# Moving the low parts of twelve weight blocks from VectorE to GpSimd in a decoder-trunk kernel

## The chip, the cores and the metric

The kernel runs on one core of a Trainium2 chip. The metric is the device time of one execution in microseconds; before the change it is 1524.93 us, the median of three runs (1524.68 to 1525.1). A profiled execution of the same kernel took 1524.4 us, of which 1522.7 us lie between its first and its last instruction.

## The reference

One inference step of a two-layer decoder trunk is computed for a prompt of 512 tokens and for 32 sample tokens (eight sequences of four), together 544 columns, with a model width of 1024. What matters here is the first mixer, a convolution layer:

```
h = rms(x, norm_mix)
a, g, mq = split(h @ w_in_a)               # 1024 -> 768, 768, 256
c = causal_dwconv(a * sigmoid(g), w, b)    # width 31, per channel
c = silu(layernorm(c))
m = mem_attend(rms(mq), mem_k, mem_v)
x = x + concat(c, m) @ w_out_a
```

After it come a gated feed-forward part, an attention layer with shared keys and values, and a second feed-forward part. All inputs and outputs are float32.

## The kernel before

**Blocks.** Every matrix product is cut into weight blocks of 1024 rows and 128 columns, which lie in SBUF as 128 partitions with 1024 elements each. The program numbers them: blocks 0 to 13 are `w_in_a` (0 to 11 alternate between a chunk of `a`, even, and the chunk of `g` that belongs to it, odd; 12 and 13 are the memory queries), and blocks from `S_MEM` = 14 on are the projections of the memory, then the output projection and the rest. To keep float32 accuracy, TensorE multiplies three times: high part of the weights by high and by low part of the activations, and low part of the weights by the high part (L532). One block of 544 columns is 48 matmuls.

**How a block gets ready.** SyncE loads it into one of four places of `w_raw` (L435; it waits until the low part of the block four places before is done). ScalarE copies it to the high part `w_hi` (L1151, `split_hi`), which waits for the load and for the matmuls of the block two before, since there are two places. VectorE subtracts, `w_lo = w_raw - w_hi` (L1600, `split_lo`), and the semaphore `w_lo_ready` counts that. TensorE waits for that count before each block.

**The order on the engines.** There is no scheduler; each engine's order is written out. In turn `s` VectorE takes the result of block `s` out of PSUM (L1669, into `glu_a`, `glu_g` or `tile_raw`), makes the low part of block `s + 2`, and does a fixed number of tap operations of the convolution (`conv(n)`, L1698 and L1700, 128x512 each). In odd turns it also makes `glu_lo` (L1712), the low part of a finished chunk of `a * sigmoid(g)`, of which ScalarE makes the high part `glu_hi` (L1236). TensorE needs both: it does 10 of the 31 taps itself as matmuls with diagonal matrices (L666, `conv_unit`), five of them beside each of the blocks 4 to 15. In odd turns `glu_ext` (L1815), `glu_new` (L1816) and a copy (L1818) follow, when the sigmoid of ScalarE is there (L1257), and then the sample tokens' taps (L1733, L1736, L1738).

**Turn 1** holds more: between blocks 1 and 2 TensorE transposes the memory rows (L612), the rows of the convolution state (L619) and of the feed-forward state (L626), VectorE copies them out of PSUM (L1827, L1831, L1837), and the squares of the memory are summed (L544).

**GpSimd** adds squares for the first norm (L2313, L2317), starts one DMA (L2337), and then waits for block 13's matmuls before it clears `mem_q_padded` (L2339) and loads cached memory keys.

Of the kernel before, what the change touches and what calls it, by code (L numbers as in the profile page):

```python
# [28 lines left out]
F32 = mybir.dt.float32  # L29
F32R = mybir.dt.float32r  # L30
I32 = mybir.dt.int32
ALU = mybir.AluOpType
# [41 lines left out]
S_MEM = S_IN + 2 * CC + MC  # L74
# [3 lines left out]
STEPS = S_FFN[1] + 68  # L78
# [8 lines left out]
def build(nc, a):  # L87
    ctx = ExitStack()
    with ctx:
        def sem(name):  # L90
            return ctx.enter_context(nc.semaphore(name))
# [4 lines left out]
        def place(name, shape, dt=F32, at=None):  # L96
            size = 4
            for n in shape[1:]:
                size *= n
            size = size + 31 & ~31  # L100
            if at is None:
                at = cursor[0]
                cursor[0] += size
            assert at + size <= nc.sbuf_usable_end, (name, at + size)
            h = nc.alloc_sbuf_tensor_at(name, shape, dt, offset=at)
            return h, at + size
# [10 lines left out]
        wraw, _ = place("w_raw", [P, 4, KD * P])  # L117
        whi, _ = place("w_hi", [P, 2, KD * P], F32R)
        wlo, _ = place("w_lo", [P, 2, KD * P], F32R)
# [113 lines left out]
        w_hi_ready, w_lo_ready = sem("w_hi_ready"), sem("w_lo_ready")  # L233
# [163 lines left out]
        def blocks_of(s):  # L397

            return HALF if S_OUT[1] <= s < S_FFN[1] else KD

        def mixed(i):

            return (0, 1, 2, 3, 6, 7, 4, 5).index(i) + 8


        turns = [(what, n) for _, what, n in sorted((g, what, n) for what in ("T", "OS", "KM", "XT", "XO", "KT", "KS", "KR")
                                                    for n, g in slots[what].items())]


        norms = [key for _, key in sorted([(8 * (s - S_B) + 12, ("tile", s)) for s, v in tiles.items()  # L410
                                           if s >= S_B and v[0] != "v"] +
                                          [(g, ("ov", h)) for h, g in slots["OV"].items()])]
# [1168 lines left out]
        def _(dve):  # L1581
# [10 lines left out]
            def split_lo(s, slot=None):  # L1592

                if slot is None:
                    if s >= STEPS:
                        return
                    slot = s % 4
                dve.wait_ge(w_hi_ready, s + 1)
                n = blocks_of(s) * P if isinstance(s, int) else KD * P
                nc.vector.tensor_tensor(wlo[:, slot % 2, 0:n], wraw[:, slot, 0:n], whi[:, slot % 2, 0:n].bitcast(F32),  # L1600
                                        ALU.subtract).then_inc(w_lo_ready, 1)
# [48 lines left out]
            for c in range(KD):  # L1650
                if c == PARAMS_AT:
                    split_lo(0)
                scaled_lo(xa_lo, xa_hi, c, xT[:, c, :], pcol("norm_mix", c), xg_hi, xg_lo, c + 1)
            split_lo(1)
            dve.wait_ge(sq_used, 8)
            root(psX[:, :, 0:HT], T, 1.0 / D, EPS, rstd[:, :])
# [134 lines left out]
            for s in range(0, S_MEM):  # L1791
                if s in tiles:
                    tile_take(s)
                    split_lo(s + 2)
                    conv(1)
                    side_conv(s)
                    tile_norm(s)
                    conv(5)
                    continue
# [502 lines left out]
        def _(pool):  # L2302
# [4 lines left out]
            def add_squares(norm, chunks=KD):  # L2307

                k = SQ[norm]
                if k:  # L2310
                    pool.wait_ge(sq_used, k)
                pool.wait_ge(sq_ready, k + 2)
                nc.gpsimd.tensor_tensor(total[:, :], sqt[:, 0, :], sqt[:, 1, :], ALU.add).then_inc(sq_used, 2)  # L2313
                for c in range(2, chunks - 1):
                    pool.wait_ge(sq_ready, k + c + 1)
                    pool.wait_ge(sq_used, k + c)
                    ins = nc.gpsimd.tensor_tensor(total[:, :], total[:, :], sqt[:, c % 2, :], ALU.add)  # L2317
                    ins.then_inc(sq_used, 1)
# [16 lines left out]

            add_squares("n0")
            pool.dma_start(a["s_conv_a"][0][:, 0:TAPS - 1 - DS, :], a["state_conv_a"][0][:, DS:, :]).then_inc(st_misc, 16)  # L2337
            pool.wait_ge(mm_done, S_MEM)
            pool.memset(qm[:, :, :], 0.0).then_inc(qm_zero, 1)  # L2339
            mem_cache_k(0)  # L2340
# [127 lines left out]
```

## Time and profile before

| | |
|---|---|
| median of three runs | 1524.93 us |
| the profiled execution | 1524.4 us |
| its span, first to last instruction | 1522.7 us |
| TensorE busy | 1419.0 us |
| VectorE busy | 953.9 us |
| ScalarE busy | 580.1 us |
| GpSimd busy | 154.3 us |
| low parts on VectorE (L1600) | 202 in 240.0 us |
| mean granted TensorE clock | 0.965 of full speed |

The sum in the prediction is made against the profiled execution, whose times run from the span's start. A granted clock of 1.00 is 2.4 GHz and of 0.50 is 1.2 GHz. In the timelines each row has a start, a time, the engine, the line and operation, and in brackets the idle time before it with what ended it. The time that a row of the timeline gives for several instructions is from the start of the first to the end of the last; starts follow each other somewhat before the end of the one before.

### The profile page before, as it was taken

To read this page: it belongs to the slowest core of one execution; us is meant where nothing else is said; L and a number is where in the kernel's file an instruction comes from. 1 tells how busy PE (TensorE), PEld (TensorE's weight loads), DVE (VectorE), ACT (ScalarE), POOL (GpSimd) and SP (SyncE) were. 2 spreads that over 40 slices of the span, in tenths; PEclk is the share of its full clock that TensorE was granted. 3 is DMA by queue.
4 is the path that set the end of the run, shared out by engine and by line. 5 is a ranking of instruction groups with operands and counts; after the bars stand their busy time and mean duration, and the time that the engine had idled before them with its cause. 6 is when DMAs were issued, how large, how long until landed. Compare 5 with 4: busy or idle time off the path is not lost.

```text
span 1522.7 us, 28281 instructions
## 1 busy us (share of the span) xinstructions
PE 1419.0 (93%) x11032; PEld 1348.2 (89%) x11032; DVE 953.9 (63%) x1825; ACT 580.1 (38%) x977; POOL 154.3 (10%) x202
## 2 busy tenths in 40 slices
PE   5899876989999999999999988888999999999997
PEld 4799874779999999999988877777899999999997
DVE  5788888556664466356776666666666536653652
ACT  3554433444342223222456545554443312221232
POOL 3000202303000000000210223320100000000001
PEclk8899987879999999999999999999999999999999
DMA  8121322214223233232222344332332322332322
GB/s 222 44 63 56 92 78 64 64 42 139 84 84 96 84 88 92 84 88 79 84 82 85 94 123 129 100 91 70 99 102 83 94 86 84 94 86 84 94 69 69
DMA packets 223216, 134.88 MB, mean 89 GB/s; under 512 B 7740, under 2 KB 216337, under 8 KB 223064
## 3 DMA queue, kind: packets, MB, share of 16 engines
q1 hardware_dynamic: 214687, 111.32, 25.3%
q0 software_dynamic: 7840, 21.89, 4.8%
q8 instruction: 72, 1.18, 0.3%
q10 hardware_dynamic: 584, 0.23, 0.1%
q14 instruction: 33, 0.26, 0.1%
HBM read 126.19 MB, written 7.85 MB: 88 GB/s over the span
## 4 chain that ended last, share of the span: by engine, by line
PE 72%; DVE 15%; ACT 7%; issue 4%; POOL 1%; ACTq 1%; DMA 0%; DVEq 0%; POOLq 0%
PE acc L532 59%; PE acc L709 3%; DVE conv_out L1698 2%; ACT w_hi L1151 2%; PE psX L666 1%; DVE w_lo L1600 1%; DVE softmax_stats L2089 1%; PE psT L666 1%; PE psX L544 1%; ACT exps L1462 1%; PE psX L796 1%; PE acc L544 1%; DVE root_row L1623 1%; ACT xa_hi L1173 1%; DVE psX L2087 1%
## 5 line engine op out<-in xcount | busy, mean ns | idle before, releaser
L532 PE MATMUL acc<-xa_hi,w_hi 128*128 128x272 f32 x1760 | 370.9, 292 | 5.4 <-DVE w_lo L1600 5.4
L532 PE MATMUL acc<-xa_hi,w_lo 128*128 128x272 f32 x1760 | 365.4, 289 | 0.0
L532 PE MATMUL acc<-xa_lo,w_hi 128*128 128x272 f32 x1760 | 364.3, 289 | 0.0
L1151 ACT ACTIVATE w_hi<-w_raw 128x1024 fp32r<-128x1024 f32 (+1 forms) x202 | 206.7, 1023 | 342.6 <-PE acc L532 311.6
L1600 DVE TENSOR_TENSOR w_lo<-w_raw,w_hi 128x1024 fp32r<-128x1024 f32 (+1 forms) x202 | 240.0, 1188 | 97.9 <-ACT w_hi L1151 96.3
L532 PEld LDWEIGHTS acc<-xa_hi,w_hi 128*128 128x128 f32 x1760 | 278.4, 190 | 11.7 <-DVE w_lo L1600 6.1
L532 PEld LDWEIGHTS acc<-xa_lo,w_hi 128*128 128x128 f32 x1760 | 278.1, 190 | 0.0
L532 PEld LDWEIGHTS acc<-xa_hi,w_lo 128*128 128x128 f32 x1760 | 276.1, 190 | 0.0
L532 PE MATMUL acc<-xb_hi,w_hi 128*128 128x272 f32 x896 | 194.6, 298 | 2.0 <-DVE xb_lo L2035 2.0
L532 PE MATMUL acc<-xb_hi,w_lo 128*128 128x272 f32 x896 | 185.7, 289 | 0.0
L532 PE MATMUL acc<-xb_lo,w_hi 128*128 128x272 f32 x896 | 185.3, 288 | 0.0
L532 PEld LDWEIGHTS acc<-xb_hi,w_hi 128*128 128x128 f32 x896 | 140.6, 189 | 13.6 <-issue 9.8
L1972 DVE TENSOR_TENSOR x_resid<-acc,x_resid 128x544 f32<-128x544 f32 (+1 forms) x72 | 52.0, 722 | 159.4 <-PE acc L532 142.9
L532 PEld LDWEIGHTS acc<-xb_lo,w_hi 128*128 128x128 f32 x896 | 141.2, 189 | 0.0
L532 PEld LDWEIGHTS acc<-xb_hi,w_lo 128*128 128x128 f32 x896 | 140.4, 189 | 0.0
L1698 DVE SCALAR_TENSOR_TENSOR conv_out<-glu_ext,params,conv_out 128x512 f32<-128x512 f32 x120 | 86.2, 772 | 0.4
L1382 ACT ACTIVATE gelu<-gate_conv,params 128x544 f32<-128x544 f32 x44 | 33.0, 750 | 133.6 <-DVE gate_conv L2015 133.5
L2015 DVE SCALAR_TENSOR_TENSOR gate_conv<-gate_ext,params,gate_conv 128x512 f32<-128x512 f32 (+1 forms) x176 | 78.8, 497 | 0.1
L2026 DVE TENSOR_TENSOR value<-acc,rstd 128x544 f32<-128x544 f32 x44 | 31.9, 724 | 53.9 <-PE acc L532 53.9
L1386 ACT ACTIVATE xb_hi<-product 128x544 f32 x44 | 29.0, 658 | 89.2 <-DVE product L2032 89.2
L2035 DVE TENSOR_TENSOR xb_lo<-product,xb_hi 128x544 f32 (+1 forms) x44 | 31.9, 725 | 40.5 <-ACT xb_hi L1386 40.5
L2313 POOL TENSOR_TENSOR square_total<-squares 128x544 f32<-128x544 f32 x5 | 7.9, 1590 | 460.7 <-ACT squares L1160 460.7
(334 smaller groups left out, 1956.7 us busy)
## 6 DMA issues: line engine op xcount, KB each, us to landing
w_raw<-in_w_up SPq DMA_DIRECT2D x88, 512.0 KB, 3.8
w_raw<-in_w_down SPq DMA_DIRECT2D x32, 512.0 KB, 3.9
w_raw<-in_w_in_a SPq DMA_DIRECT2D x14, 512.0 KB, 3.8
w_raw<-in_w_down SPq DMA_DIRECT2D x16, 384.0 KB, 3.4
w_raw<-in_w_kv SPq DMA_DIRECT2D x12, 512.0 KB, 3.9
k_pages<-in_cache_k POOLq DMA_DIRECT2D x96, 64.0 KB, 2.2
v_pages<-in_cache_v SPq DMA_DIRECT2D x96, 64.0 KB, 2.2
w_raw<-in_w_mem_kv SPq DMA_DIRECT2D x8, 512.0 KB, 3.9
```

What stands on the lines that cost most here:

```text
L532: last = nc.tensor.matmul(acc[slot][:, c, 0:n], w, x[:, k, c * n:(c + 1) * n], start=(k == 0 and q == 0), stop=(k == kb - 1 and q == 2))
L544: last = nc.tensor.matmul(out[:, c, 0:n], w, sqt[:, k % 2, c * n:(c + 1) * n], start=first, stop=final)
L666: last = nc.tensor.matmul(tap_sum(j)[:, c, :], diag[:, u % 2, d, :], x[:, at:at + NPR // 2], start=(i + q == 0), stop=(i == NPT - 1 and q ...
L709: last = nc.tensor.matmul(acc[s % 2][:, c, 0:HT], w, x[:, k, c * HT:(c + 1) * HT], start=(i == 0 and q == 0), stop=(i == KD - 1 and q == 2))
L1151: nc.scalar.activation(whi[:, slot % 2, 0:n], wraw[:, slot, 0:n], ACT.Copy).then_inc(w_hi_ready, 1)
L1382: nc.scalar.activation(gel[:, :], gcv[:, :], ACT.Gelu_apprx_tanh, bias=pcol_at("ffn_conv_b", q)).then_inc(gelu_ready, 1)
L1600: nc.vector.tensor_tensor(wlo[:, slot % 2, 0:n], wraw[:, slot, 0:n], whi[:, slot % 2, 0:n].bitcast(F32), ALU.subtract).then_inc(w_lo_ready, 1)
L1698: ins = nc.vector.scalar_tensor_tensor(out=o, in0=src, scalar=w, in1=o, op0=ALU.mult, op1=ALU.add)
L1972: nc.vector.tensor_tensor(x, acc[b_][:, :, 0:HT], x, ALU.add).then_inc(acc_free, 1)
L2015: ins = nc.vector.scalar_tensor_tensor(out=o, in0=x, scalar=w, in1=o, op0=ALU.mult, op1=ALU.add)
L2026: nc.vector.tensor_tensor(val[:, :].rearrange("p (c n) -> p c n", c=2), acc[(sc + 1) % 2][:, :, 0:HT], rstd[:, :].rearrange("p (c n) -> p ...
L2035: nc.vector.tensor_tensor(lo, prod[:, :], hi.bitcast(F32), ALU.subtract).then_inc(ulo_ready, 1)
```

## The change

The low parts of blocks 2 to 13 are subtracted by GpSimd, in its program right after the first norm's squares and the DMA of the state, in place of VectorE. `split_lo` leaves these blocks out; for block 14 VectorE waits in addition until block 13's low part is counted, so that the count stays in order. GpSimd waits for each block's high part, and before block 2 for the low parts of blocks 0 and 1.

```
             def split_lo(s, slot=None):
 
                 if slot is None:
-                    if s >= STEPS:
+                    if s >= STEPS or 2 <= s < S_MEM:
                         return
                     slot = s % 4
+                if isinstance(s, int) and s == S_MEM:
+                    dve.wait_ge(w_lo_ready, S_MEM)
                 dve.wait_ge(w_hi_ready, s + 1)
...
             add_squares("n0")
             pool.dma_start(a["s_conv_a"][0][:, 0:TAPS - 1 - DS, :], a["state_conv_a"][0][:, DS:, :]).then_inc(st_misc, 16)
+            for s in range(2, S_MEM):
+                pool.wait_ge(w_hi_ready, s + 1)
+                if s == 2:
+                    pool.wait_ge(w_lo_ready, 2)
+                nc.gpsimd.tensor_tensor(wlo[:, s % 2, :], wraw[:, s % 4, :], whi[:, s % 2, :].bitcast(F32),
+                                        ALU.subtract).then_inc(w_lo_ready, 1)
             pool.wait_ge(mm_done, S_MEM)
```

The order on VectorE before, in turns 0 and 1 (`glu_a` and `glu_g` are the results of blocks 0 and 1 out of PSUM, `w_lo` the low parts of blocks 2 and 3):

```order
L1669 TENSOR_TENSOR glu_a<-acc,rstd 128x544
L1600 TENSOR_TENSOR w_lo<-w_raw,w_hi 128x1024
L1669 TENSOR_TENSOR glu_g<-acc,rstd 128x544
L1600 TENSOR_TENSOR w_lo<-w_raw,w_hi 128x1024
L1815 TENSOR_TENSOR glu_ext<-glu_a,glu_s 128x512
L1816 TENSOR_TENSOR glu_new<-glu_a,glu_s 128x32
L1818 COPY glu_ext<-glu_new 128x8x4
L1827 COPY mem_t<-psT 128x512 x4
```

The same place now (line numbers after the change are higher by two):

```order
L1671 TENSOR_TENSOR glu_a<-acc,rstd 128x544
L1671 TENSOR_TENSOR glu_g<-acc,rstd 128x544
L1817 TENSOR_TENSOR glu_ext<-glu_a,glu_s 128x512
L1818 TENSOR_TENSOR glu_new<-glu_a,glu_s 128x32
L1820 COPY glu_ext<-glu_new 128x8x4
L1829 COPY mem_t<-psT 128x512 x4
```

Both low parts are gone from this place; in the other turns up to 11 one goes in the same way, from between the PSUM read and the taps. GpSimd's order now, around the place where they have come in:

```order
L2319 TENSOR_TENSOR square_total<-square_total,squares 128x544 x5
L2339 DMA out_s_conv_a<-in_state_conv_a 8x2x9984
L2344 TENSOR_TENSOR w_lo<-w_raw,w_hi 128x1024 x12
L2347 MEMSET mem_q_padded 128x2304
```

The memset followed directly on the DMA before. The orders of TensorE, ScalarE and SyncE are the same in both programs.

## Rows read from the trace of the kernel before

**Rows 1.** The page's busy times, all engines: busy us, share, instructions
```profile
PE 1419.0 (93%) x11032; PEld 1348.2 (89%) x11032; DVE 953.9 (63%) x1825; ACT 580.1 (38%) x977; POOL 154.3 (10%) x202
```
**Rows 2.** Timelines of PE, DVE and ACT around turn 1
```profile
42.85 0.42 PE L532 MATMUL acc<-xa_hi,w_lo 128*128 128x272 f32 x2
...
43.31 0.72 DVE L1669 TENSOR_TENSOR glu_g<-acc,rstd 128x544 f32<-128x544 f32 x1
45.70 1.22 DVE L1600 TENSOR_TENSOR w_lo<-w_raw,w_hi 128x1024 fp32r<-128x1024 f32 x1 [1.67 <-ACT w_hi L1151]
46.84 0.68 DVE L1815 TENSOR_TENSOR glu_ext<-glu_a,glu_s 128x512 f32<-128x512 f32 x1
47.66 0.18 DVE L1818 COPY glu_ext<-glu_new 128x32 f32<-128x32 f32 x1
...
44.06 0.66 ACT L1257 ACTIVATE glu_s<-glu_g 128x544 f32<-128x544 f32 x1 [0.96 <-DVE glu_g L1669]
44.63 1.04 ACT L1151 ACTIVATE w_hi<-w_raw 128x1024 fp32r<-128x1024 f32 x1
```
**Rows 3.** Timeline of POOL: two additions of a later stage
```profile
240.72 1.57 POOL L2359 TENSOR_TENSOR square_total<-square_total,conv_out 128x544 f32<-128x544 f32 x1 [0.17 <-POOL square_total L2359]
...
248.77 1.34 POOL L2359 TENSOR_TENSOR square_total<-square_total,conv_out 128x544 f32<-128x544 f32 x1 [4.74 <-DVE conv_out L1698]
```
**Rows 4.** Groups of POOL, shapes apart: busy us, mean ns
```profile
L2339 POOL MEMSET mem_q_padded<- 128x2304 f32 x1 | 2.0, 2017 | 143.6 <-PE acc L532 143.6
...
L2303 POOL MEMSET ones<- 128x128 f32 x1 | 0.2, 204 | 0.3 <-POOLq L2457 0.3
```
**Rows 5.** Timeline of DVE: one tap operation that met the addition at 240.72
```profile
241.03 1.81 DVE L1698 SCALAR_TENSOR_TENSOR conv_out<-glu_ext,params,conv_out 128x512 f32<-128x512 f32 x1
```
**Rows 6.** Groups of DVE from 40 to 166 us: busy us, mean ns
```profile
L1698 DVE SCALAR_TENSOR_TENSOR conv_out<-glu_ext,params,conv_out 128x512 f32<-128x512 f32 x58 | 40.0, 746 | 0.2
```
**Rows 7.** Timelines of ACT, PE and DVE in turns 2 and 3
```profile
71.21 1.04 ACT L1151 ACTIVATE w_hi<-w_raw 128x1024 fp32r<-128x1024 f32 x1
...
75.36 0.41 PE L532 MATMUL acc<-xa_hi,w_hi 128*128 128x272 f32 x2
...
75.79 0.72 DVE L1669 TENSOR_TENSOR glu_g<-acc,rstd 128x544 f32<-128x544 f32 x1
...
77.11 1.04 ACT L1151 ACTIVATE w_hi<-w_raw 128x1024 fp32r<-128x1024 f32 x1
...
80.10 0.51 PE L666 MATMUL psT<-glu_hi,tap_diagonals 128*128 128x256 f32 x2 [0.83 <-DVE glu_lo L1712]
```
**Rows 8.** Timelines of ACT, DVE and PE in turns 10 and 11
```profile
144.57 1.06 ACT L1151 ACTIVATE w_hi<-w_raw 128x1024 fp32r<-128x1024 f32 x1
...
147.88 0.68 DVE L1721 TENSOR_TENSOR conv_out<-psT,conv_out 128x512 f32<-128x512 f32 x1
...
154.09 0.72 DVE L1669 TENSOR_TENSOR glu_g<-acc,rstd 128x544 f32<-128x544 f32 x1 [0.31 <-PE acc L532]
156.48 1.23 DVE L1600 TENSOR_TENSOR w_lo<-w_raw,w_hi 128x1024 fp32r<-128x1024 f32 x1 [1.67 <-ACT w_hi L1151]
...
155.41 1.04 ACT L1151 ACTIVATE w_hi<-w_raw 128x1024 fp32r<-128x1024 f32 x1
156.36 0.64 ACT L1236 ACTIVATE glu_hi<-glu_ext 128x542 fp32r<-128x542 f32 x1
...
159.72 0.50 PE L666 MATMUL psT<-glu_hi,tap_diagonals 128*128 128x256 f32 x2 [0.50 <-DVE glu_lo L1712]
```
**Rows 9.** Timeline of DVE, start of turn 12
```profile
165.99 0.72 DVE L1669 TENSOR_TENSOR tile_raw<-acc,rstd 128x544 f32<-128x544 f32 x1
```
**Rows 10.** Timeline of PE: the two idle times followed by a lower clock
```profile
48.62 1.97 PE L612 MATMUL psT<-consts,mem_rows 128*128 128x128 f32 x8 [4.48 <-DVE mem_t L1827]
...
172.95 0.50 PE L666 MATMUL psT<-glu_hi,tap_diagonals 128*128 128x256 f32 x2 [2.48 <-ACT tap_diagonals L1249]
```
**Rows 11.** Stretches of 2 us; PEclk is the granted TensorE clock
```profile
48.00:50.00 2.00, 1.38 (x7) 1.38 (x8) 1.39 (x3) 0.72 (x2) 0.00 (x0) 0.50 0.87 251
173.00:175.00 2.00, 2.00 (x11) 2.00 (x12) 1.97 (x4) 1.18 (x4) 0.00 (x0) 0.63 0.02 6
```

## The prediction

> **What bounds the kernel now.** I read the page first: TensorE is busy for 1419.0 of 1522.7 us [rows 1], so work taken off VectorE pays only where TensorE waits for VectorE. The changed blocks lie between 40 and 166 us, and there I read the timelines of all four engines side by side. The reader is to see three places. In turn 1 the chain runs over VectorE: it waits 1.67 us for the high part of block 3, makes the low part, and only then comes to `glu_ext` at 46.84 and to the copies that TensorE's transposes wait for; TensorE is idle for 4.48 us until 48.62 [rows 2, 10]. In turns 3 to 11 TensorE is nearly full and waits once in two blocks, for `glu_lo`: 0.83 us before 80.10, 0.50 before 159.72 [rows 7, 8]. From turn 11 on VectorE is the chain: after `glu_lo` it has no pause until it reads block 12 at 165.99 [rows 9], with ScalarE's next high part and TensorE's next taps behind it. So what counts is when `glu_ext` starts in turn 1 and when `glu_lo` ends in the odd turns.
>
> **What a low part costs on GpSimd.** Its addition of 544 elements takes 1.34 us alone [rows 3]. The two memsets give a fixed part of about 0.1 us: (2017 - 204) / (2304 - 128) is 0.83 ns an element, and 204 less 128 x 0.83 leaves 0.10 [rows 4]. The addition then costs 1.24 / 544 = 2.28 ns an element, and 1024 elements 0.1 + 2.33 = **2.43 us**, twice the 1.22 of VectorE [rows 2]. No row shows GpSimd writing this rounded type, so I keep both ends: 1.74 us if only the memset's 0.83 ns were to grow over the further 480 elements, and 4.86, twice my value, if the type were slow. I take 2.43, since an operation of the same kind and engine is the nearest row.
>
> The Trainium skill (GPSIMD Engine Reference, section 3.1) states 4497 ns for such an operation on 2048 elements, and so an estimate of 2.25 us here, 0.18 less; with six such terms (below) the sum would be -1.9 us, 1523.0. No run here shows it yet.
>
> **What it costs VectorE.** A tap operation takes 0.75 us alone [rows 6]. The one that began at 241.03, while an addition ran from 240.72 to 242.29, took 1.81 and ended at 242.84, 0.55 after the addition [rows 3, 5]. It did not run slowly beside it, it stood until GpSimd was through. I therefore let each VectorE operation with two inputs in SBUF end 0.58 us after a GpSimd subtraction that it meets (542 elements in place of 512), and leave those that read PSUM, and the sums, undisturbed.
>
> The same skill gives the rule (SBUF — State Buffer, section on who interferes with whom): a VectorE instruction with two SBUF inputs blocks against a GpSimd one that reads SBUF. A picture of shared bandwidth would give the gain of the no-block rival below. By that rule, the trace agrees.
>
> **The sum, in order of time.**
> Turn 0: block 2's low part goes from between the two PSUM reads. TensorE ends block 1 at 42.85 + 0.42 = 43.27, and `glu_g` starts at 43.31 at the earliest: nothing gained.
> Turn 1: `glu_ext` now waits for the sigmoid alone, 44.06 + 0.66 = 44.72, and starts at 44.75 in place of 46.84: **2.09 us** earlier [rows 2]. Block 3's subtraction runs from 45.8 to 48.2 and meets copies out of PSUM. The whole chain of transposes, squares and memory scaling after it moves by 2.09.
> Turns 2 and 3: most of that is lost again. Block 4's high part ends at 72.25 - 2.09 = 70.16, its low part at 0.1 + 2.43 later, 72.69; TensorE asks for it at 75.36 - 2.09 = 73.27, so it is in time by 0.6. But VectorE's two taps stand until it ends: 72.69 + 0.55 + 0.71 (the first tap ends 0.55 after the block, the second takes 0.71 more) = 73.95, when `glu_g` starts, 0.25 later than 75.79 less the shift. Block 5's high part then ends at 73.95 + 1.32 + 1.04 = 76.31, its low part at 78.84, and `glu_lo` 0.58 later, 79.42. Before, a low part of 1.14 stood in that place. TensorE's tap starts at 79.5 in place of 80.10: **0.6 us** are left of the 2.09 [rows 7].
> Turns 5, 7, 9, 11: the high part ends at 156.45; before, VectorE then took 1.14 for the low part, two taps and `glu_lo`, and TensorE went on at 159.72. Now the two taps are done during the wait, and `glu_lo` stands until 156.55 + 2.43 = 158.98 and ends at 159.56, and with a slower hand-over at 159.6. I take 0.05 us each turn, **0.2 us** in four: what the wait gives is what the block takes [rows 8].
> Even turns: block 12's subtraction ends at 145.63 + 0.1 + 2.43 = 148.2. VectorE meanwhile takes sums and PSUM reads, which do not stand; its taps would begin at 147.5 (147.88 less 1.14, plus the 0.72 of L1721) and stand 0.7 us, with 1.14 saved. VectorE also has 0.31 us of idle time before `glu_g` as cover [rows 8]. If that cover were gone, a long block would delay `glu_g` by its excess. Nothing gained or lost.
> Turn 12 on: the added wait of VectorE is for block 13, subtracted by 159 us, 7 us before VectorE comes to that wait; nothing is held up behind it. The operations behind the twelve on GpSimd, the memset and DMAs, wait for block 13's matmuls until 179.21 anyway (143.6 us of idle time, rows 4). SyncE's loads of blocks 6 to 17 start up to 2.6 us later each and are needed two blocks, some 20 us, after. The shift at 165.99 is carried to the end.
>
> Sum: -0.6 - 0.2 = **-0.8 us**. The profiled execution of 1524.4 becomes 1523.6; the median stood 0.5 higher, so 1524.93 becomes **1524.1**. About 0.2%, 3 us, is what a measurement of this kernel can tell from no change.
>
> **The rivals.**
> *No blocking of these shapes.* Then turn 1 keeps 2.09, TensorE's waits for `glu_lo` go (0.83 and four times 0.5), and VectorE reads block 12 some 1.4 us earlier still: -6.3, 1518.6. Rows 5 speak against it. 5%.
> *The clock holds in turn 1.* TensorE's idle time shrinks from 4.48 to 2.4 us. After 4.48 us the granted clock was 0.50 (1.2 GHz) and eight transposes took 1.97 us; after 2.48 us it fell too, to 0.63 on average [rows 10, 11]. If 2.4 just does not do it, up to half of the transposes' 8 us is saved, some 3 us with VectorE's copies between: -3.8, 1521.1. The 2.48 speaks against it. 10%.
> *The copy at 47.66 is caught.* It would start at 45.57, and block 3's subtraction at 45.77. Should that order turn, and should copies stand as well, turn 1 gains nothing and loses 0.5: 2.6 more than the forecast, +1.8, 1526.7. No row shows it. 5%.
> *GpSimd is slower, and `glu_lo` becomes the bound.* Each us above 2.43 counts in the low parts of blocks 4 and 5 and once in each of four more odd turns, six times. It decides from 2.43 + 0.8/6 = 2.56 us on, and passes +3 us at 3.07. At 4.86 it gives -0.8 + 6 x 2.43 = +13.8, 1538. For it: the type is new on this engine. Against it: VectorE takes 1.22 us for 1024 with the type, in line with its other pairs. 12%.
> That the change does not do what it says can be left out: the order shows the twelve on GpSimd.
>
> **How the numbers follow.** The forecast has 68%, and spreads with its own duration: 1.74 us gives about -4 (1521.0), as the waits of TensorE cap the gain. Slower by over 3 us: 10% of the last rival's 12. Faster by over 3 us: 5% and 8% from the first two, 2% from a short duration, 15%. Same: 75%. The range takes in the clock case and, on the other side, a duration of 3 us (+2.6): 1521.0 to 1527.5, and leaves out the no-block rival and the slow type.
>
> **What would show it.** The subtractions on GpSimd take 2.3 to 2.5 us. `glu_ext` of turn 1 starts near 44.8; TensorE's first tap starts near 79.5, the one of turn 11 near 158.9, and block 12 is read near 165.2. Tap operations and `glu_lo` of up to 2.3 us appear on VectorE, with its busy time nearly unchanged though twelve operations have gone. The prediction is wrong if `glu_lo` in turn 3 ends before 79 (no blocking), if the granted clock stays at 1.00 in 47 to 60 us, or if a subtraction takes 3 us or more.

## The result, and the profile after

The changed kernel takes 1526.92 us (median of 20 runs, 1524.6 to 1530.12), the kernel before 1524.78 (20 runs). The ratio is 1.0015, with an interval of 1.0008 to 1.0021: **slower by 2.1 us**, 1.2 to 3.2. Forecast were 0.8 us less. The time lies in the stated range and under the bound of 0.2%, but it moved the other way. The profiled execution took 1529.04 us with a span of 1527.1, which is 2.1 us more than the median of its kind, so its end says little; what follows is read from distances inside the stage. Of all runs below, one of experiment 10 took 2137 us and is left out of its ratio.

The page's first lines, of the changed kernel (line numbers from L1600 on are two higher, and eight behind the new loop of GpSimd):

```profile
span 1527.1 us, 28283 instructions
...
PE 1421.6 (93%) x11032; PEld 1349.7 (88%) x11032; DVE 958.0 (63%) x1813; ACT 580.3 (38%) x977; POOL 184.0 (12%) x214
```

Against [rows 1], GpSimd has the twelve subtractions more, and VectorE, with twelve operations fewer, is busy for 4 us longer. Turn 1, timelines of DVE and ACT, against [rows 2]:

```profile
45.69 0.72 DVE L1671 TENSOR_TENSOR glu_g<-acc,rstd 128x544 f32<-128x544 f32 x1 [1.85 <-PE acc L532]
47.20 0.69 DVE L1817 TENSOR_TENSOR glu_ext<-glu_a,glu_s 128x512 f32<-128x512 f32 x1 [0.79 <-ACT glu_s L1257]
...
46.45 0.66 ACT L1257 ACTIVATE glu_s<-glu_g 128x544 f32<-128x544 f32 x1 [1.78 <-DVE glu_g L1671]
```

`glu_ext` follows `glu_g` by 1.51 us, where it was 3.53: the gain of turn 1 is there, 2.02 us. Turns 2 and 3, timelines of POOL, DVE and PE, against [rows 7]:

```profile
71.58 2.40 POOL L2344 TENSOR_TENSOR w_lo<-w_raw,w_hi 128x1024 fp32r<-128x1024 f32 x1 [21.09 <-ACT w_hi L1151]
78.18 2.35 POOL L2344 TENSOR_TENSOR w_lo<-w_raw,w_hi 128x1024 fp32r<-128x1024 f32 x1 [4.21 <-ACT w_hi L1151]
...
71.89 2.37 DVE L1702 TENSOR_SCALAR conv_out<-glu_ext,params 128x512 f32<-128x512 f32 x1
75.75 0.72 DVE L1671 TENSOR_TENSOR glu_g<-acc,rstd 128x544 f32<-128x544 f32 x1
78.69 2.43 DVE L1714 TENSOR_TENSOR glu_lo<-glu_ext,glu_hi 128x542 fp32r<-128x542 f32 x1 [2.22 <-ACT glu_hi L1236]
...
81.17 0.57 PE L666 MATMUL psT<-glu_hi,tap_diagonals 128*128 128x256 f32 x2 [2.25 <-DVE glu_lo L1714]
```

The reader is to see two VectorE operations that end with GpSimd's subtraction: the `TENSOR_SCALAR` of 71.89, which I had let run free, ends 0.28 us after its subtraction, and `glu_lo` 0.59 us after the next. TensorE waits 2.25 us for the latter, where it was 0.83. Turns 9 to 12, the same engines, against [rows 8, 9]:

```profile
149.10 2.39 POOL L2344 TENSOR_TENSOR w_lo<-w_raw,w_hi 128x1024 fp32r<-128x1024 f32 x1 [6.51 <-ACT w_hi L1151]
...
149.22 2.32 DVE L1740 TENSOR_SCALAR conv_out<-conv_out,params 128x32 f32<-128x32 f32 x1
151.57 0.72 DVE L1671 TENSOR_TENSOR glu_a<-acc,rstd 128x544 f32<-128x544 f32 x1
...
158.03 0.72 DVE L1671 TENSOR_TENSOR glu_g<-acc,rstd 128x544 f32<-128x544 f32 x1
160.96 2.48 DVE L1714 TENSOR_TENSOR glu_lo<-glu_ext,glu_hi 128x542 fp32r<-128x542 f32 x1 [0.90 <-ACT glu_hi L1236]
...
169.77 0.72 DVE L1671 TENSOR_TENSOR tile_raw<-acc,rstd 128x544 f32<-128x544 f32 x1
```

A `TENSOR_SCALAR` on 32 columns takes 2.32 us. In the same place of the kernel before it takes 0.24 (timeline of DVE):

```profile
145.82 0.24 DVE L1738 TENSOR_SCALAR conv_out<-conv_out,params 128x32 f32<-128x32 f32 x1
```

Its place is the end of turn 9, between the sample sums and the read of block 10. The 0.31 us of idle time before `glu_g` are gone. The granted clock in turn 3 (the last three columns of each row are PEclk, DMA share, GB/s):

```profile
78.00:80.00 2.00, 0.92 (x8) 0.70 (x6) 1.31 (x1) 1.82 (x6) 1.82 (x1) 1.00 0.00 0
80.00:82.00 2.00, 0.83 (x5) 0.83 (x6) 1.97 (x3) 0.00 (x0) 0.54 (x1) 0.86 0.10 28
82.00:84.00 2.00, 2.00 (x11) 2.00 (x11) 1.97 (x4) 0.70 (x2) 0.00 (x0) 0.50 0.82 242
```

It falls to 0.50 (1.2 GHz) right after the long wait, for some 3.4 us; before, it was 1.00 from 61 us to 173.

### The profile page after: what moved, and what is told of

It reads as the page before. It is cut to its first block, busy times and chain, and to the rows that moved or that the text cites. A ratio compares the mean times of both kernels' runs of the same rounds, so it can differ in the third digit from the quotient of the medians.

```text
span 1527.1 us, 28283 instructions
## 1 busy us (share of the span) xinstructions
PE 1421.6 (93%) x11032; PEld 1349.7 (88%) x11032; DVE 958.0 (63%) x1813; ACT 580.3 (38%) x977; POOL 184.0 (12%) x214
## 4 chain that ended last, share of the span: by engine, by line
PE 72%; DVE 16%; ACT 7%; issue 3%; POOL 1%; ACTq 1%; DMA 0%; DVEq 0%; POOLq 0%
PE acc L532 59%; PE acc L709 3%; DVE conv_out L1700 2%; ACT w_hi L1151 2%; DVE softmax_stats L2091 1%; PE psT L666 1%; PE psX L666 1%; PE psX L544 1%; ACT exps L1462 1%; DVE glu_lo L1714 1%; PE psX L796 1%; PE acc L544 1%; DVE w_lo L1602 1%; DVE root_row L1625 1%; DVE probs L2124 1%
## 5 line engine op out<-in xcount | busy, mean ns | idle before, releaser
L1602 DVE TENSOR_TENSOR w_lo<-w_raw,w_hi 128x1024 fp32r<-128x1024 f32 (+1 forms) x190 | 225.4, 1186 | 87.9 <-ACT w_hi L1151 86.3
L2037 DVE TENSOR_TENSOR xb_lo<-product,xb_hi 128x544 f32 (+1 forms) x44 | 31.9, 725 | 40.5 <-ACT xb_hi L1386 40.5
```

The lines of the kernel that those rows point to most:

```text
L2037: nc.vector.tensor_tensor(lo, prod[:, :], hi.bitcast(F32), ALU.subtract).then_inc(ulo_ready, 1)
```

## How the experiments are read

Three traces of the kernel before and four of the changed one (below) showed that the start of `glu_g` in turn 1 lies anywhere from 43.3 to 46.1 us, with the place of the half-clock stretches, and the time from block 12's read to the end between 1353.2 and 1357.3. The second does not follow the change. The first may: it is 43.24 to 44.85 us in the four traces with block 3 on VectorE, and 44.77 to 47.05 in the ten with block 3 on GpSimd. The delay is there before the first moved subtraction begins, so nothing in the traces leads from the change to it; it is taken up below. To keep both out, each trace is cut at the starts of `glu_g` in turns 1, 3, 5, 7, 9 and 11 and of `tile_raw` in turn 12, all from the timeline of DVE; the last column is their sum, "the stage".

| kernel, blocks on GpSimd | 1 to 3 | 3 to 5 | 5 to 7 | 7 to 9 | 9 to 11 | 11 to 12 | stage |
|---|---|---|---|---|---|---|---|
| before, none | 32.48 | 18.58 | 19.91 | 19.91 | 19.90 | 11.90 | 122.68 |
| before, second trace | 32.49 | 18.57 | 19.90 | 19.92 | 19.90 | 11.91 | 122.69 |
| before, third trace | 32.67 | 18.58 | 19.90 | 19.91 | 19.91 | 11.91 | 122.88 |
| changed, 2 to 13 | 30.06 | 21.22 | 20.52 | 20.27 | 20.27 | 11.74 | 124.08 |
| changed, second trace | 30.15 | 19.71 | 20.50 | 20.28 | 20.27 | 11.74 | 122.65 |
| changed, third trace | 30.09 | 21.10 | 20.51 | 20.27 | 20.27 | 11.76 | 124.00 |
| changed, fourth trace | 30.05 | 21.25 | 20.51 | 20.28 | 20.28 | 11.73 | 124.10 |
| 3 | 30.51 | 18.58 | 19.91 | 19.90 | 19.91 | 11.92 | 120.73 |
| 2, 4, ..., 12 | 33.28 | 18.65 | 20.72 | 20.52 | 20.53 | 11.99 | 125.69 |
| 3, 5, ..., 13 | 30.55 | 19.71 | 19.72 | 19.75 | 19.77 | 11.73 | 121.23 |
| 2 to 13, constant in place of the bias | 30.05 | 21.25 | 20.51 | 20.27 | 20.26 | 11.68 | 124.02 |
| 2 to 13, that operation left out | 30.10 | 21.21 | 19.75 | 19.74 | 19.73 | 11.46 | 121.99 |
| 2 to 4 and 6 to 13 | 30.06 | 18.66 | 20.50 | 20.27 | 20.27 | 11.73 | 121.49 |
| 3, 7, 9, 11, 13 | 29.53 | 18.59 | 19.76 | 19.74 | 19.73 | 11.74 | 119.09 |

In the first column the half-clock stretch of turn 1 (from 47 to 52 us on) is some 13.7 us long in the traces of 30.5 us and over, and 10.2 in the others. What makes it shorter was not separated, so this column holds about 1 us of clock. The ratio given with each experiment is the one on record for its runs; it is not the quotient of the two medians, and differs from it by up to about 0.1% (experiment 10).

All experiments that split the blocks use one table of blocks:

```
+GP = (3,)
...
-                    if s >= STEPS or 2 <= s < S_MEM:
+                    if s >= STEPS or s in GP:
...
-                if isinstance(s, int) and s == S_MEM:
-                    dve.wait_ge(w_lo_ready, S_MEM)
+                if isinstance(s, int) and s - 1 in GP:
+                    dve.wait_ge(w_lo_ready, s)
...
-            for s in range(2, S_MEM):
+            for s in GP:
                 pool.wait_ge(w_hi_ready, s + 1)
-                if s == 2:
-                    pool.wait_ge(w_lo_ready, 2)
+                if s - 1 not in GP:
+                    pool.wait_ge(w_lo_ready, s)
```

## Experiment 1: block 3 alone

The edit is the one above.

> Only block 3's low part is made by GpSimd, the other eleven stay on VectorE. Theory A (the cost lies in the blocks that meet VectorE operations with an input in SBUF, single-input ones too): block 3 meets only copies out of PSUM, so turn 1 keeps its gain and nothing is paid later: glu_ext of turn 1 starts 1.5 us after glu_g in place of 3.53, every later turn as before, total about 2.0 us less than before, 1522.8. Theory B (the earlier start of turn 1 is worth nothing, since TensorE or its clock takes it back in any case): 1524.8, no change.

Measured: 1522.02 us against 1525.18, ratio 0.9973 (0.9963 to 0.9983). The stage is 120.73, 1.95 less than before, all of it in turn 1. Timelines of DVE and POOL in turn 1:

```profile
45.00 0.72 DVE L1672 TENSOR_TENSOR glu_g<-acc,rstd 128x544 f32<-128x544 f32 x1
46.51 0.69 DVE L1818 TENSOR_TENSOR glu_ext<-glu_a,glu_s 128x512 f32<-128x512 f32 x1 [0.79 <-ACT glu_s L1258]
...
47.45 2.35 POOL L2345 TENSOR_TENSOR w_lo<-w_raw,w_hi 128x1024 fp32r<-128x1024 f32 x1 [11.67 <-ACT w_hi L1152]
```

So the gain of turn 1 is real and is carried to the end; theory B falls. The whole run gained somewhat more than the stage (2.6 to 5.6 us by the interval, against 1.95); the stage does not explain that excess, and it stays open.

## Experiment 2: the even blocks alone

`GP = (2, 4, 6, 8, 10, 12)`; the rest of the edit is the one above.

> Only the even blocks 2, 4, ..., 12 are made by GpSimd. Theory A: no gain in turn 1; the 128x32 tensor_scalar after the sample sums (0.24 us alone) stands for about 2.3 us in turns 5, 7 and 9, and the 128x512 one of turn 2 for 2.4 in place of 0.54; glu_g to glu_g of the odd turns from 7 on grows from 19.9 to 20.3 us or a little more; total +1.5 to +2.5 us, 1526.3 to 1527.3. Theory B (even turns cost nothing, as the prediction on record had it; all of the loss is in the odd turns and the clock): odd turns 19.9 us apart, total within 0.5 us of before.

Measured: 1527.5 us, ratio 1.0011 (1.0002 to 1.002); stage 125.69, 3.01 more than before, where theory A had 1.5 to 2.5 in all. Timeline of DVE, turns 2, 3 and 9:

```profile
72.64 2.38 DVE L1703 TENSOR_SCALAR conv_out<-glu_ext,params 128x512 f32<-128x512 f32 x1
76.52 0.72 DVE L1672 TENSOR_TENSOR glu_g<-acc,rstd 128x544 f32<-128x544 f32 x1
...
148.12 2.33 DVE L1741 TENSOR_SCALAR conv_out<-conv_out,params 128x32 f32<-128x32 f32 x1
150.48 0.72 DVE L1672 TENSOR_TENSOR glu_a<-acc,rstd 128x544 f32<-128x544 f32 x1
```

Turn 2 pays 0.80 us, and turns 5 to 10 pay 0.81, 0.61 and 0.63 for each pair, an odd turn and the even one behind it. The last two can be worked out: the operation stands for 2.33 - 0.24 = 2.09 us, VectorE is relieved of a subtraction of 1.14, and 0.31 of idle time covers part of the rest: 0.64.

## Experiment 3: the odd blocks alone

`GP = (3, 5, 7, 9, 11, 13)`.

> Only the odd blocks 3, 5, ..., 13 are made by GpSimd. Theory A: turn 1 gains 2.0 us, turn 3 loses about 1.1 (glu_lo ends 5.4 us after glu_g starts in place of 4.25), turns 5 to 11 gain 0.1 to 0.16 each (glu_lo ends 5.41 in place of 5.57 us after glu_g); total -1.0 to -1.5, 1523.5, and up to 1.7 us more where the granted clock falls after the longer wait of turn 3. Theory B (odd turns carry the loss): total +1.5 to +2.5, 1526.3 to 1527.3.

Measured: 1522.54 us, ratio 0.9986 (0.9977 to 0.9995); stage 121.23, 1.45 less. Turn 3 costs 1.13, and turns 5 to 11 gain 0.19, 0.16, 0.13 and 0.17. Together with experiment 2 this makes +3.01 - 1.45 = +1.56, where all twelve blocks measured +1.40 in the profiled execution. That these lie so close is in part luck: the +1.40 hold some 1.2 us less of half clock in turn 1 and 1.4 us more in turn 3, which the two experiments do not have. Timeline of DVE in turn 11:

```profile
154.60 0.72 DVE L1672 TENSOR_TENSOR glu_g<-acc,rstd 128x544 f32<-128x544 f32 x1 [0.32 <-PE acc L533]
157.54 2.47 DVE L1715 TENSOR_TENSOR glu_lo<-glu_ext,glu_hi 128x542 fp32r<-128x542 f32 x1 [0.90 <-ACT glu_hi L1237]
```

`glu_lo` ends 5.41 us after `glu_g` starts, where [rows 8] give 159.66 - 154.09 = 5.57. The 0.32 us of idle time before `glu_g`, gone in the changed kernel, are there again.

## Experiments 4 and 5: the 128x32 operation

Experiment 4 keeps all twelve blocks on GpSimd and adds a constant 0 in place of the bias column, to see whether it is the read of that column that stands. The sample tokens' convolution is then without its bias, here and in experiment 5.

```
-                link(nc.vector.tensor_scalar(o, o, pcol("conv_a_b", j), None, ALU.add))
+                link(nc.vector.tensor_scalar(o, o, 0.0, None, ALU.add))
```

> All twelve blocks on GpSimd as in the change, and the 128x32 tensor_scalar of the sample taps adds the constant 0 in place of the bias column (the bias of the sample tokens' convolution is left out). Theory A1 (what stands is the read of the scalar column from SBUF): the operation takes 0.24 us again in turns 5, 7 and 9, the odd turns come 19.8 us apart, total 1.0 to 1.3 us less than the changed kernel, about 1525.7. Theory A2 (a tensor_scalar stands whatever its scalar is): it takes 2.3 us again, total as the changed kernel, 1526.9. Theory B (it is not this operation that matters): 1526.9 whatever it takes.

Measured: 1528.1 us, ratio 1.0019 (1.001 to 1.0028), and the same distances as the changed kernel. Timeline of DVE at the end of turn 5:

```profile
107.87 1.19 DVE L1739 TENSOR_REDUCE conv_out<-sample_tap_products 128x32 f32<-128x992 f32 x1
109.09 2.32 DVE L1741 TENSOR_SCALAR conv_out<-conv_out 128x32 f32<-128x32 f32 x1
111.44 0.72 DVE L1672 TENSOR_TENSOR glu_a<-acc,rstd 128x544 f32<-128x544 f32 x1
```

Without the column it takes 0.18 us alone and 2.32 beside a subtraction. A2 holds, A1 falls. Experiment 5 leaves the operation out:

```
                 settle()
-                link(nc.vector.tensor_scalar(o, o, pcol("conv_a_b", j), None, ALU.add))
-                settle()
```

> All twelve blocks on GpSimd, and the 128x32 tensor_scalar after the sample sums left out (the bias of the sample tokens' convolution is not added). If that operation is the price of the even turns: the PSUM read after it goes on undisturbed, the first tap of turns 6, 8 and 10 stands 0.7 us at most, glu_g to glu_g from turn 5 to 11 is 19.7 to 19.8 us in place of 20.3 to 20.5, total about 2 us below the changed kernel, 1525. Rival (whatever comes next is blocked in its place, the price only moves on to the taps): 20.2 us or more, total as the changed kernel, 1526.9.

Measured: 1526.04 us against 1525.44, ratio 0.9999 (0.9987 to 1.0011). The distances of turns 5 to 11 fall from 20.5 and 20.3 to 19.75, 19.74 and 19.73. Timelines of POOL and DVE:

```profile
107.47 2.40 POOL L2343 TENSOR_TENSOR w_lo<-w_raw,w_hi 128x1024 fp32r<-128x1024 f32 x1 [6.52 <-ACT w_hi L1152]
...
107.59 0.72 DVE L1672 TENSOR_TENSOR glu_a<-acc,rstd 128x544 f32<-128x544 f32 x1
108.23 0.68 DVE L1724 TENSOR_TENSOR conv_out<-psT,conv_out 128x512 f32<-128x512 f32 x1
108.94 6.13 DVE L1701 SCALAR_TENSOR_TENSOR conv_out<-glu_ext,params,conv_out 128x512 f32<-128x512 f32 x8
```

Here is the even turn as the prediction had it. The two reads of PSUM run at their full speed while GpSimd subtracts; only the first tap stands, 0.74 us (eight taps in 6.13 us, 5.39 before). The distances are those of experiment 3, where no even block is on GpSimd. So this operation of 0.24 us is the whole price of the even turns 6 to 10, give or take the 0.24 us that leaving it out saves by itself, and what comes after it was not blocked in its place.

## Experiments 6 to 8: both kernels again

No edit; each of the two kernels as it is, in five executions.

> The changed kernel once more, for a second trace. If the structure found is right, the distances inside the stage repeat to 0.1 us where the granted clock is the same (20.5, 20.3, 20.3 us from glu_g to glu_g, turns 5 to 11), while the time up to glu_g of turn 1 may lie anywhere between 43 and 46.5 us, with the place of the half-clock stretches. If the start of glu_g in turn 1 is late because of the change, it is 45 us or later again.

> The kernel before once more, for a second trace. 19.9 us from glu_g to glu_g, 122.7 us from glu_g of turn 1 to the read of block 12, give or take the clock between the two. If the start of glu_g in turn 1 is set by chance, it can be 45 to 46 us here too; if the change sets it, 43.3.

> The changed kernel a third time. The two traces so far have turn 3 with and without a half-clock stretch (21.22 and 19.71 us). If chance decides, either again; nothing between the two. The other turns 20.5, 20.3, 20.3 us.

> The kernel before a third time: turn 3 without a half-clock stretch (18.58 us), 19.9 us each for the three after it, and glu_g of turn 1 at 43 to 44 us, or 45 to 46 if its place is chance.

> The changed kernel a fourth time, as the third: 21.2 or 19.7 us in turn 3.

Measured, one execution each: changed 1522.58, 1526.71 and 1527.85 us, before 1524.17 and 1524.34. `glu_g` of turn 1 starts at 44.77, 45.47 and 46.09 in the changed kernel, and at 43.64 and 44.85 in the one before. The delay goes with the clock: in the first trace of the changed kernel it was 0.50 from 33.7 to 40.5 us, in the first of the kernel before it was 1.00 there. Such a stretch between 33 and 42 us is in all ten traces with block 3 on GpSimd and in two of the four others, and the first of the moved subtractions begins only at 43.46 in the profiled execution, when the delay is already there. Whether chance or the changed program puts it there stays open.

It matters for the total. On average the spans of the four traces of the changed kernel are 2.2 us longer than those of the three of the kernel before: 1.6 of that lie before `glu_g` of turn 1, 1.0 in the stage, and -0.3 behind it.

Turn 3 comes in two forms. In the second trace of the changed kernel the wait is the same and the clock holds; timeline of PE, then stretches:

```profile
80.35 0.50 PE L666 MATMUL psT<-glu_hi,tap_diagonals 128*128 128x256 f32 x2 [2.26 <-DVE glu_lo L1714]
```

```profile
80.00:82.00 2.00, 1.65 (x13) 1.65 (x14) 1.93 (x4) 0.64 (x2) 0.00 (x0) 1.00 0.46 128
82.00:84.00 2.00, 2.00 (x19) 2.00 (x18) 1.93 (x5) 0.76 (x3) 0.00 (x0) 1.00 0.45 134
```

The next `glu_g` comes after 19.71 us, against 21.10 to 21.25 in the other three traces: the fall of the clock costs **1.4 to 1.5 us**. It came in five of the six traces with a wait of 2.2 to 2.3 us (four of the changed kernel, experiments 4 and 5), and in none of the eight with 1.73 or less.

## Experiment 9: all but block 5

`GP = (2, 3, 4, 6, 7, 8, 9, 10, 11, 12, 13)`.

> Eleven blocks on GpSimd, block 5 alone back on VectorE. If block 5 makes TensorE's 2.2 us wait of turn 3 and the fall of the clock after it: that wait is 1.6 us as with the even blocks alone, the granted clock stays at 1.00 through turn 3, glu_g of turn 3 to glu_g of turn 5 is 18.65 us (21.22 or 19.71 in the changed kernel), the later turns stay at 20.5, 20.3 and 20.3, total 1.1 to 2.6 us below the changed kernel, about 1525. Rival (the fall of the clock goes with the other blocks or with chance): 20.2 us there.

Measured: 1524.11 us against 1524.83, ratio 0.9999 (0.999 to 1.0008). Timeline of PE in turn 3:

```profile
81.49 0.51 PE L667 MATMUL psT<-glu_hi,tap_diagonals 128*128 128x256 f32 x2 [1.20 <-DVE glu_lo L1715]
```

The wait is 1.20 us (less than the 1.6 I had expected), the clock stays at 1.00, turn 3 takes 18.66 us. Without block 5 both the long wait and the fall behind it are gone: 21.2 less 18.66 is 2.5 us. Block 5 does not make them alone: in experiment 3, with block 5 but not block 4 on GpSimd, the wait was 1.73 us and the clock held. The even turns keep their price. The stage is 1.19 us shorter than before, and the run time the same within 1.5 us.

## Experiment 10: only the blocks that pay

`GP = (3, 7, 9, 11, 13)`.

> Blocks 3, 7, 9, 11 and 13 on GpSimd, the others on VectorE (block 5 and the even ones left out). Theory A (each block has its own price by what it meets): from glu_g of turn 1 to the read of block 12 the sum of the single terms seen so far, -1.93 in turn 1, 0 in turns 2 and 3, -0.19, -0.16, -0.13 and -0.17 in turns 5, 7, 9 and 11, so 120.1 us in place of 122.68; total 2.6 us below before, about 1522.2. Rival (the small gains of the odd turns need the even blocks or block 5, or are chance): 120.7 us as with block 3 alone, total 1522.8.

Measured: 1521.03 us against 1525.44, ratio 0.9982 (0.9968 to 0.9995). The stage is 119.09, 3.6 less than before; 1 us of that is the clock's share in turn 1 (29.53 against 30.51 us in experiment 1, which is the same program up to there). Turns 5 to 11 give 0.15, 0.17, 0.17 and 0.16, as the single terms said. It is faster than both kernels; between it and block 3 alone the run times decide nothing (the intervals overlap), and only the distances of turns 5 to 12 do.

## Why the prediction was wrong

**Turn 0 and 1: right.** 2.09 us forecast, 2.02 seen and 1.95 carried through (experiment 1). `glu_ext` itself started at 47.20 and not near 44.8, as `glu_g` came at 45.69 and not at 43.31. Turn 0 was not tested by itself.

**The subtraction: right.** 2.43 us forecast, 2.35 to 2.41 where nothing was in its way; no row shows an extra cost of the type on this engine. The Trainium skill's figure (GPSIMD Engine Reference, section 3.1) gave an estimate of 2.25, a little low by these rows.

**Odd turns: right, and a little better.** `glu_lo` ends 0.59 us after the block (160.46 + 2.39 = 162.85, and 163.44), with 0.58 forecast; of gain 0.05 was forecast and 0.13 to 0.19 seen. The forecast's own rows gave 0.10 (159.66 less 159.56).

**Even turns: the step that failed.** The prediction said that VectorE "meanwhile takes sums and PSUM reads, which do not stand", and "nothing gained or lost". The PSUM reads do not stand (experiment 5), and the sums are over within 0.1 us of GpSimd's start. Between the two is a 128x32 `TENSOR_SCALAR`, which I took for part of the sums, and it stands: +0.6 to +0.8 for a pair of turns, three times, less 0.13 to 0.19 for each odd turn (experiments 2 to 5). The two experiments add up to +1.57 us for these turns, and the changed kernel has +1.34, where -0.15 had been forecast. My rule, that only operations with two SBUF inputs stand, came from one row of that kind. The trace of the kernel before held a row against it, which I had not used (timelines of POOL and DVE):

```profile
262.57 1.34 POOL L2359 TENSOR_TENSOR square_total<-square_total,conv_out 128x544 f32<-128x544 f32 x1 [12.46 <-DVE conv_out L1698]
...
259.72 0.62 DVE L1881 TENSOR_SCALAR exps<-exps,softmax_stats 128x256 f32<-128x256 f32 x2
...
262.60 1.72 DVE L1881 TENSOR_SCALAR exps<-exps,softmax_stats 128x256 f32<-128x256 f32 x2
```

A pair of `TENSOR_SCALAR` that takes 0.62 us takes 1.72 when it meets GpSimd's addition. With that row the 128x32 operation would have been let stand: a low part of 2.43 us in place of one of 1.14, some 1.3 us in each of the even turns 6, 8 and 10, less 0.31 of cover. The forecast would have been a loss of over 2 us.

**Turns 2 and 3: mis-sized.** The same operation, on 512 columns, put `glu_g` of turn 3 late by 0.80 and not 0.25 (experiment 2). Block 5 costs 1.13 (experiment 3), where the forecast had 1.2. Together the two leave nothing of turn 1's gain, where 0.6 us were to be left.

**The clock: seen for the wrong place.** I weighed it for turn 1 alone, where the wait gets shorter. In turn 3, where my own sum made TensorE's wait longer (by some 1.5 us on 0.83), I did not ask. The wait became 2.25 us, and in most traces 1.4 to 1.5 us of half clock follow it. In turn 1 the rival with the clock came true in part: TensorE's idle time fell from 4.48 to 2.47 us, and the half-clock stretch became 3.5 us shorter, worth about 1 us, in eight of the ten traces with block 3 on GpSimd and in none of the four others. Experiments 1 and 3, which kept the long stretch, are up to there the same program as experiment 10, which did not. So chance has a share in it, and how much is the change's was not separated.

The balance of the profiled execution: -2.42 (turns 1 and 2, a gain of 2.0 less 0.8, and the rest, 1.2, put down to the clock), +2.64 (turns 3 and 4: 1.13 for block 5, 0.07 as with the even blocks, 1.44 of clock), +1.34, -0.16 = +1.40 in the stage. Without the two clock terms it is +1.2, where -0.8 was forecast: 1.5 of the 2.0 us between them lie in turns 5 to 10, 0.6 in turns 1 to 3, and turn 11 gave 0.1 more than forecast.

The 2.1 us of the medians are more by 0.7, which the interval of 1.2 to 3.2 does not set apart from it. But in the three other kernels with blocks 2 and 3 both on GpSimd (experiments 4, 5 and 9) the run time, by the ratio, is also worse than the stage alone would have it, by 0.5 to 1.6 us, and in experiments 1 to 3 it is better, by 0.7 to 2.2. The start of `glu_g` in turn 1 does not sort them so: it is late in experiments 1 and 3 too. So the stage's loss is explained; what lies outside the stage is of the same size, and stays open.

The rival that stood for a loss (a slow type on GpSimd) was not what happened, though its mechanism, VectorE's wait for GpSimd deciding the turn, was.

## What to carry to other kernels

Work moved from VectorE to GpSimd is paid for by whatever VectorE does at that moment: list each operation of VectorE that can fall into the window, down to the smallest, and charge it the rest of GpSimd's operation unless a row shows that its kind runs on. Search the whole trace for such rows, other stages too. Move the pieces singly and only where VectorE is in PSUM reads or in a wait: one block of twelve gave all of turn 1's 2 us, and the even ones took 3 back. When a sum makes a wait of TensorE longer, price the lower clock behind it as well (1.4 to 1.5 us here, behind five waits of six).

## What the runs showed of the hardware

An operation with one SBUF input stands too: the 128x512 `TENSOR_SCALAR` took 2.37 us in place of 0.54, ending 0.28 us after the subtraction, and the 128x32 one 2.32 in place of 0.24, with a column or a constant as its scalar alike. The read of PSUM with a second input in SBUF (0.72 and 0.68 us, experiment 5) and the copy out of PSUM (two in 1.29 us at 48.25 in the changed kernel, as before) kept their times. The Trainium skill (SBUF — State Buffer, section on who interferes with whom) names `tensor_scalar` among the operations that can contend, for its two-port modes, and says that outside those modes an instruction with at most one SBUF input does not. Groups of DVE in the kernel before, shapes apart (busy us, mean ns):

```profile
L1600 DVE TENSOR_TENSOR w_lo<-w_raw,w_hi 128x1024 fp32r<-128x1024 f32 x186 | 229.0, 1231 | 93.0 <-ACT w_hi L1151 91.4
L1600 DVE TENSOR_TENSOR w_lo<-w_raw,w_hi 128x512 fp32r<-128x512 f32 x16 | 10.9, 684 | 4.9 <-ACT w_hi L1151 4.9
L2120 DVE TENSOR_SCALAR probs<-exps,softmax_stats 128x512 f32<-128x512 f32 x6 | 2.9, 480 | 0.0
L2120 DVE TENSOR_SCALAR probs<-exps,softmax_stats 128x128 f32<-128x128 f32 x6 | 1.7, 278 | 0.0
```

Each further column costs `TENSOR_SCALAR` (480 - 278) / 384 = 0.53 ns, and the subtraction with two inputs (1231 - 684) / 512 = 1.07, twice as much; in a short operation the fixed part hides it. This fits such a mode, and so the trace agrees with the first of the two statements. The reads of PSUM above have one input in SBUF and kept their times, so it agrees with the second too.

GpSimd is held up as well when VectorE began first. The subtraction that began at 88.59 us, just after a tap operation of VectorE at 88.56, took 2.96 us in place of 2.40, and so in all five traces with the fall of the clock in turn 3 (2.96 or 2.97).
